# The level products of four recurrent heads: one group of 96 small matmuls on TensorE in place of two groups of 48

## The reference, cut to what matters

```python
def step(state, inp):
    qn, kn, vn, fn = inp
    b = jnp.cumsum(fn, axis=2)
    inter = jnp.einsum('bhtk,bhkv->bhtv', qn * jnp.exp(b), state)
    diff = b[:, :, :, None, :] - b[:, :, None, :, :]
    decay = jnp.exp(jnp.where(causal, diff, 0.0)) * causal_f
    a = jnp.einsum('bhtk,bhtsk,bhsk->bhts', qn, decay, kn)
    o = inter + jnp.einsum('bhts,bhsv->bhtv', a, vn)
    b_last = b[:, :, -1:, :]
    state = (jnp.exp(b_last[:, :, 0, :])[..., None] * state
             + jnp.einsum('bhsk,bhsv->bhkv', kn * jnp.exp(b_last - b), vn))
```

## Time and profile before

| | |
|---|---|
| median of 3 runs | 2510.53 us (2509.77 to 2511.0) |
| the profiled execution's own time | 2509.97 us |
| its span in the trace | 2508.7 us |
| TensorE busy | 2502.2 us of the span |
| VectorE busy | 1358.9 us |
| ScalarE busy | 918.4 us |
| GpSimd busy | 149.5 us |
| the four heads that the change touches | 140 to 350 us of the span |

### The profile page before, as it was taken

One profiled execution on the slowest core, in us unless ns is written; L12 is line 12 of the kernel. 1 busy time (PEld: TensorE's weight loads), 2 busy tenths in 40 slices (PEclk: granted clock), 3 DMA queues, 4 the chain that ended last, 5 costly groups with the idle time before them and its releaser, 6 DMA issues.

```text
span 2508.7 us, 31305 instructions
## 1 busy us (share of the span) xinstructions
PE 2502.2 (100%) x12614; PEld 2075.9 (83%) x12614; DVE 1358.9 (54%) x2248; ACT 918.4 (37%) x1259; POOL 149.5 (6%) x195
## 2 busy tenths in 40 slices
PE   9999999999999999999999999999999999999999
PEld 8888888888888888888888888888888888888888
DVE  7557744567544555655443363485256555665425
ACT  6633325333332222322232253443344344544423
POOL 0011110012100000000001103200000000000001
PEclk9999999999999999999999999999999999999999
DMA  5333333333335666666443232236222243433432
GB/s 192 110 96 95 96 105 95 95 95 100 100 93 164 213 218 214 218 212 212 149 161 110 93 101 93 93 101 178 92 76 76 85 125 101 113 106 112 178 101 101
DMA packets 213633, 317.95 MB, mean 127 GB/s; under 512 B 66736, under 2 KB 69680, under 8 KB 212464
## 3 DMA queue, kind: packets, MB, share of 16 engines
q1 hardware_dynamic: 208592, 312.55, 40.2%
q0 software_dynamic: 4320, 2.99, 0.5%
q10 hardware_dynamic: 576, 0.42, 0.1%
HBM read 295.43 MB, written 8.39 MB: 121 GB/s over the span
## 4 chain that ended last, share of the span: by engine, by line
PE 100%; ACT 0%; DVE 0%; issue 0%; ACTq 0%; DVEq 0%
PE bank L366 94%; PE bank L1449 1%; PE bank L1450 1%; PE bank L1451 1%; PE bank L798 0%; PE bank L857 0%; PE bank L782 0%; PE bank L860 0%; PE bank L825 0%; PE bank L1841 0%; PE bank L1955 0%; PE bank L1953 0%; PE bank L1954 0%; PE bank L467 0%; ACT OT L2266 0%; PE bank L472 0%
## 5 line engine op out<-in xcount | busy, mean ns | idle before, releaser
L366 PE MATMUL bank<-XH,WH 128*128 128x512 f32 (+1 forms) x2776 | 1078.7, 390 | 0.0
L366 PE MATMUL bank<-XH,WL 128*128 128x512 f32 (+1 forms) x2776 | 1074.5, 389 | 0.0
L366 PE MATMUL bank<-XL,WH 128*128 128x512 f32 (+1 forms) x2776 | 1074.0, 389 | 0.0
L418 DVE TENSOR_TENSOR WL<-RAW,WH 128x1024 fp32r<-128x1024 f32 x430 | 530.1, 1234 | 760.6 <-ACT WH L395 760.0
L395 ACT CAST WH<-RAW 128x1024 fp32r<-128x1024 f32 x430 | 450.1, 1048 | 1113.4 <-PE bank L366 1102.2
L366 PEld LDWEIGHTS bank<-XH,WL 128*128 128x128 f32 x2776 | 521.0, 188 | 108.1 <-DVE WL L418 0.2
L366 PEld LDWEIGHTS bank<-XH,WH 128*128 128x128 f32 x2776 | 521.0, 188 | 107.7 <-ACT WH L395 0.2
L366 PEld LDWEIGHTS bank<-XL,WH 128*128 128x128 f32 x2776 | 521.2, 188 | 107.1 <-issue 0.5
L366 PE MATMUL bank<-WH,XL 128*128 128x512 f32 x384 | 149.4, 389 | 0.0
L366 PE MATMUL bank<-WH,XH 128*128 128x512 f32 x384 | 149.4, 389 | 0.0
L366 PE MATMUL bank<-WL,XH 128*128 128x512 f32 x384 | 149.4, 389 | 0.0
(11 more groups left out here) (351 smaller groups left out, 1882.7 us busy)
## 6 DMA issues: line engine op xcount, KB each, us to landing
RAW<-in_w_in SPq DMA_DIRECT2D x303, 512.0 KB, 3.8
AST<-in_w_ada SPq DMA_DIRECT2D x192, 256.0 KB, 4.1
RAW<-in_w_o SPq DMA_DIRECT2D x32, 512.0 KB, 3.7
RAW<-in_w_gate SPq DMA_DIRECT2D x32, 512.0 KB, 3.6
RAW<-in_w_out SPq DMA_DIRECT2D x32, 512.0 KB, 3.7
RAW<-in_w_a SPq DMA_DIRECT2D x16, 512.0 KB, 4.2
RAW<-in_w_b SPq DMA_DIRECT2D x16, 512.0 KB, 4.3
PT<-ZT SPq DMA_DIRECT2D x256, 32.0 KB, 1.9
```

Source lines behind the costliest of these rows:

```text
L366: ins = nc.tensor.matmul(bank[b][:, cols], l, r[:, cols], start=first, stop=final)
L418: nc.vector.tensor_tensor(low_of(m), RAW[:, m % NRAW], high_of(m).bitcast(F32), ALU.subtract).then_inc(lo.sem, lo.step(m))
```

## The change

For heads 0 to 3 (`JOINED`) all eight levels are computed at slot 8 in one group. Levels 0 to 3 share one bank and levels 4 to 7 the other. Levels 3 and 5 are packed into 64 columns each instead of 256 (`half_of_tiles`), so that a bank's 512 columns suffice: 192 + 256 + 64, and 256 + 64 + 64 + 128. Their takes become four instructions of 32 or 16 partitions (`take_half_of_tiles`) instead of one of 128. The rows of levels 5, 6 and 7 move to rows 4, 5 and 6 of YA, which the convolution writes only in the second half of the heads. The takes of levels 0 to 3 move behind the product group. VectorE's number of slots stays the same. Heads 4 to 7 keep the two groups.

```diff
@@ -754,7 +754,13 @@
     XX4 = sb("XX4", [512], F32, W0 + 98560)
     XQ = sb("XQ", [16, 48], F32, W0 + 98560)
 
-    def level_rows(lev):
+    JOINED = range(4)
+
+    def level_rows(hh, lev):
+        if hh in JOINED and lev > 4:
+            if hh < 4:
+                return YA[:, lev - 1]
+            return O[:, lev] if hh == 4 else (LF, KK, Q)[lev - 5][:, hh - 5]
         return XX4[:, :] if lev == 7 else XX[:, {2: 2, 3: 1, 4: 0, 5: 1, 6: 2}[lev]]
 
     QUERIES = XX[:, 1]
@@ -793,26 +799,36 @@
             T.wait_ge(dve, (yield dve, ("xl", hh, lev)))
             for n in range(16):
                 y = 32 * n % 128
-                t = level_rows(lev)[:, 32 * n:32 * n + 32]
+                t = level_rows(hh, lev)[:, 32 * n:32 * n + 32]
                 c = slice(at + 16 * n, at + 16 * n + 16)
                 ins = nc.tensor.matmul(b[y:y + 32, c].rearrange("p (n x) -> p n x", x=h), t,
                                        late(t, lev), start=True, stop=True, tile_position=(0, y))
             return ins
 
...
@@ -825,21 +841,33 @@
                 ins = nc.tensor.matmul(b[:, CH[c]], KT[:, c], VN[:, c, 128 * i:128 * i + 128], start=True, stop=True)
             ins.then_inc(side.sem, side.step(("sums", hh)))
 
-        yield from idle(3)
-        b = yield from product_bank((0, 1))
-        yield from pairs_and_diagonal(b)
-        b = yield from product_bank((2, 3))
-        yield from within_tiles(2, b, 0)
-        ins = yield from within_tiles(3, b, 256)
-        ins.then_inc(side.sem, side.step(("prod", hh, 3)))
-        yield
-        yield from idle(3)
-        b = yield from product_bank((4, 5))
-        yield from within_tiles(4, b, 0)
-        yield from within_tiles(5, b, 256)
-        b = yield from product_bank((6, 7))
-        yield from across_tiles(b)
-        ins = yield from across_halves(b)
+        if hh in JOINED:
+            yield from idle(7)
+            b = yield from product_bank((0, 1, 2, 3))
+            yield from pairs_and_diagonal(b)
+            yield from within_tiles(2, b, 192)
+            yield from half_of_tiles(3, b, 448)
+            b = yield from product_bank((4, 5, 6, 7))
+            yield from within_tiles(4, b, 0)
+            yield from half_of_tiles(5, b, 256)
+            yield from across_tiles(b, 320)
+            ins = yield from across_halves(b, 384)
+        else:
+            yield from idle(3)
+            b = yield from product_bank((0, 1))
+            yield from pairs_and_diagonal(b)
+            b = yield from product_bank((2, 3))
+            yield from within_tiles(2, b, 0)
+            ins = yield from within_tiles(3, b, 256)
+            ins.then_inc(side.sem, side.step(("prod", hh, 3)))
+            yield
+            yield from idle(3)
+            b = yield from product_bank((4, 5))
+            yield from within_tiles(4, b, 0)
+            yield from within_tiles(5, b, 256)
+            b = yield from product_bank((6, 7))
+            yield from across_tiles(b, 0)
+            ins = yield from across_halves(b, 64)
         ins.then_inc(side.sem, side.step(("prod", hh, 7)))
         yield
         yield from idle(3)
@@ -921,6 +949,7 @@
     def hgrn_dve(i, hh):
         half = hh // 4
         lf, kk, q, r = LF[:, i], KK[:, i], Q[:, i], RR[:, :]
+        early = ("prod", hh, 7 if hh in JOINED else 3)
 
         def take_diagonal():
             b = bank[banks["prod", hh, 0]]
...
+        def take_half_of_tiles(lev):
+            h = 1 << (lev - 1)
+            at = 448 if lev == 3 else 256
+            b = bank[banks["prod", hh, lev]]
+            V.wait_ge(side, (yield side, ("prod", hh, 7)))
+            V.wait_ge(dve, (yield dve, ("take", hh, lev - 1)))
+            for y in range(0, 128, 32):
+                rows = slice(y, y + 32)
+                if lev == 5:
+                    ins = nc.vector.tensor_copy(ATD[y:y + 16, :, y + 16:y + 32],
+                                                b[y:y + 16, at:at + 64].rearrange("p (c x) -> p c x", c=4))
+                    continue
+                src = b[rows, at:at + 64].rearrange("p (c n x) -> p c n x", c=4, x=h)
+                msk = late(MASK[rows, lev, rows], lev).unsqueeze(1).broadcast_to([32, 4, 16 // h, h])
+                ins = nc.vector.copy_predicated(
+                    ATD[rows, :, rows].rearrange("p c (n x) -> p c n x", x=2 * h)[:, :, :, h:], msk, src)
+            ins.then_inc(dve.sem, dve.step(("take", hh, lev)))
+
...
@@ -985,7 +1033,8 @@
             V.wait_ge(act, (yield act, ("up", hh, lev)))
             V.wait_ge(ev_d, (yield ev_d, (("q", half), i)))
             if lev > 4:
-                V.wait_ge(side, (yield side, ("prod", hh, 3)))
+                if hh not in JOINED:
+                    V.wait_ge(side, (yield side, ("prod", hh, 3)))
             elif hh % 4:
                 V.wait_ge(dve, (yield dve, ("o", hh - 1)))
             if lev == 1:
...
@@ -1012,10 +1061,10 @@
             nc.vector.tensor_tensor(vw(lf)[:, :, h:], vw(lf)[:, :, h:],
                                     vw(lf)[:, :, h - 1:h].broadcast_to([128, n, h]), ALU.add
                                     ).then_inc(dve.sem, dve.step(("b", hh, lev)))
-            if lev == 5:
+            if lev == 5 and hh not in JOINED:
                 yield from take_diagonal()
                 yield from take_pairs()
-            if lev == 6:
+            if lev == 6 and hh not in JOINED:
                 yield from take_within(2)
                 yield from take_within(3)
             yield
@@ -1032,18 +1081,33 @@
         nc.vector.transpose(ZK[:, :, :], KEYS[:, BEFORE_END].rearrange("p (b x) -> p b x", x=32)
                             ).then_inc(dve.sem, dve.step(("kt", hh)))
         yield
-        yield from take_within(4)
-        yield from take_within(5)
+        if hh in JOINED:
+            yield from take_diagonal()
+            yield from take_pairs()
+            yield from take_within(2)
+        else:
+            yield from take_within(4)
+            yield from take_within(5)
         yield
         V.wait_ge(act, (yield act, ("up", hh, 8)))
         V.wait_ge(side, (yield side, ("prod", hh, 7)))
         nc.vector.tensor_tensor(QUERIES[:, AFTER_START], q[:, AFTER_START], EE[:, 0, AFTER_START], ALU.mult
                                 ).then_inc(dve.sem, dve.step(("queries", hh)))
-        yield from take_across(6)
-        yield
-        yield from take_across(7)
-        yield
-        yield
+        if hh in JOINED:
+            yield from take_half_of_tiles(3)
+            yield from take_within(4)
+            yield
+            yield from take_half_of_tiles(5)
+            yield from take_across(6)
+            yield
+            yield from take_across(7)
+            yield
+        else:
+            yield from take_across(6)
+            yield
+            yield from take_across(7)
+            yield
+            yield
         V.wait_ge(side, (yield side, ("sums", hh)))
         b = bank[banks["sums", hh]]
         nc.vector.tensor_copy(ST[:, 0], b[:, CH[0]]).then_inc(dve.sem, dve.step(("state", hh, 0)))
```

More of the change, by code:

```diff
@@ L800, in within_tiles, with half_of_tiles, across_tiles, across_halves @@
             return ins
-        def across_tiles(b):
+        def half_of_tiles(lev, b, at):
+            h = 1 << (lev - 1)
+            T.wait_ge(dve, (yield dve, ("xl", hh, lev)))
+            for n in range(16):
+                y = 32 * (n % 4)
+                t = level_rows(hh, lev)[:, 32 * n:32 * n + 32]
+                c = slice(at + 16 * (n // 4), at + 16 * (n // 4) + 16)
+                nc.tensor.matmul(b[y:y + 32, c].rearrange("p (n x) -> p n x", x=h), t,
+                                 late(t, lev), start=True, stop=True, tile_position=(0, y))
+        def across_tiles(b, at):
             T.wait_ge(dve, (yield dve, ("xl", hh, 6)))
-            x = level_rows(6)
+            x = level_rows(hh, 6)
             for n in range(8):
                 c, p = n // 2, n % 2
-                tile_product(b, 64 * p + 32 * (c % 2), 32 * (c // 2),
+                tile_product(b, 64 * p + 32 * (c % 2), at + 32 * (c // 2),
                              x[:, 64 * n:64 * n + 32], x[:, 64 * n + 32:64 * n + 64])
-        def across_halves(b):
+        def across_halves(b, at):
             T.wait_ge(dve, (yield dve, ("xl", hh, 7)))
-            x = level_rows(7)
+            x = level_rows(hh, 7)
             for n in range(8):
                 c, p = n // 2, n % 2
-                ins = tile_product(b, 64 * (c % 2) + 32 * p, 64 + 64 * (c // 2),
+                ins = tile_product(b, 64 * (c % 2) + 32 * p, at + 64 * (c // 2),
                                    x[:, 64 * n - 32 * p:64 * n - 32 * p + 32], x[:, 128 * c + 64:128 * c + 128])
@@ L931, in take_diagonal @@
                 V.wait_ge(pool, (yield pool, "at0"))
-            V.wait_ge(side, (yield side, ("prod", hh, 3)))
+            V.wait_ge(side, (yield side, early))
             for y in range(0, 128, 32):
@@ L952, in take_within @@
```

(15 more changed lines are left out.)

## The result

The changed kernel takes 2516.9 us, the median of 10 runs (2515.29 to 2519.88), against 2510.12 for the kernel before in the same session (10 runs, 2509.77 to 2511.02). The ratio is 1.0027, with a 95% interval of 1.0017 to 1.0037: slower by 6.8 us, where 1.2 less was forecast. The scatter has grown as well, from 1.3 to 4.6 us.

What follows compares the result with a forecast made beforehand. TensorE's queue length was taken as the bound (busy 2502.2 of 2508.7 us). The profiled 2509.97 less 1.2 for four heads' change-overs gives 2508.8; with the median 0.56 above that execution, 2509.3 was forecast, range 2506.8 to 2513.2.

Steps and rivals of the forecast that it cites:

- The likeliest case: Whole kernel: joining saves 1.2 us on TensorE, for a median of 2509.3 us; chance 0.71.
- The change-over of 0.30 us a head: TensorE: exit of the first product group and entry of the second go, 0.10 + 0.11 + 0.09 us; 1.2 for four heads.
- The sum: Profiled execution 2509.97 us less 1.2 is 2508.8; the runs' median lies 0.56 above that execution, so 2509.3.
- rival 2: TensorE's instruction fetch too slow for joined groups of 384 records: 2511.7 us with two heads, 2514.1 with four; chance 0.11.
- no margin: Instruction fetch: a packet takes 1.2 us to move and lasts 1.2 us at 19 ns a matmul, so the durations are equal.
- The present groups show no such pause though some must cross a border: Argument against fetch starvation: the two groups at 1.70 us, for example, show no pause, though some groups must cross packet borders.
- Rival 1: TensorE's product groups: nothing saved, the change-over pauses reappear inside the joined group, costing 2.5 us; time 2510.5; chance 0.12.
- Rival 3: VectorE finishes level 7 or the states too late for TensorE's output matmuls: 2511.6 us, or 2518.5 for every head; chance 0.04.
- The costs of its takes: VectorE: four level 3 takes at 0.30 us, four level 5 copies at 0.22 to 0.30; 1.0 to 1.4 us more a head.
- Slots, bank waits, SyncE's and GpSimd's queues: Head stays 17 slots, no DMA added, key transfers and clearing no later, bank waits covered by slack: no cost on TensorE.

Runs made afterwards that it cites:

- the version with two groups: Changed kernel, but TensorE issues levels 0 to 3 at slot 4 and 4 to 7 at slot 8 again: 2510.37 us, ratio 1.0 to the kernel before.

## Why the prediction was wrong

**The likeliest case.** The change-over of 0.30 us a head was right in kind: the unpaused joined groups cost 2.14 to 2.46 us against 2.48, so they save 0.02 to 0.34 a head, on average 0.2. Joined where no border troubles them, four heads saved 0.8 us inside their groups where 1.2 was said; the median's 1.0 is within the interval of no change.

**Where the sum failed.** The sum, 2509.97 less 1.2, put the instruction supply at nothing. The text knew of it as rival 2, with a chance of 0.11 and a price that was too low, "at most one packet time, 1.2 us". The range did not even cover that price: it ends at 2513.2, and rival 2 with all four heads stood at 2514.1. I had worked out the time in which the DMA engines move a packet, and set it against the 1.2 us in which a packet is used up. From there the two seemed equal, hence "no margin" but a small price. The runs show that the packet is the smaller part of a refill. From its landing to the next instruction are 1.3 to 1.5 us more, and it starts late besides. The next instruction came 3.3 to 4.9 us after the start of the group, while within the burst the block in hand is used up after 1.4 to 1.8. Inside a group the pause is 1.9 to 3.0 us, 1.6 to 2.5 times the price that I gave as its highest. The second missing term is the clock: nothing in the trace of before shows TensorE pausing, so I did not price what a pause does to it. Its half clock costs 1.0 to 1.65 us and stood behind 8 of 14 pauses. In the profiled execution head 0 costs 2.9 us more than before, head 3 1.75 and the half clock 1.6, while heads 1 and 2 save 0.6: 5.7 together, against a span 5.5 longer. The median lies 1.3 us further off; no trace shows those executions, and their pauses or half clock are not known singly.

**Where the chances failed.** "The present groups show no such pause though some must cross a border" was taken for evidence. It is none: a group of 192 instructions can cross at most one border, and the block behind it is already there. Only a group longer than 256 can use up the next one as well within its burst. The arithmetic for this stood in the text (192 against 384), and should have given this rival more than 0.11, and the position of each group in the stream could have been counted. Two of four heads, as it said, were struck.

The page of the Trainium skill, "Runtime: NRT & Kernel Launch" (Instruction fetch mechanics), was read as undecided between a store of 2048 instructions and two lines of 256. The pauses decide it for this kernel: each comes exactly one block after the border whose refill is awaited, so no more than one block was in hand. The same section says that the fetch is hidden since instructions are dispatched more slowly than the blocks are filled. The trace disagrees for this stream, in which 192 instructions leave in 1.0 us and a refill takes 3.3 us or more.

**Rival 1** falls by the traces: it wanted a joined group at 2.5 us, and the unpaused ones cost 2.14 to 2.46, 2.27 on average. The times alone can't tell it from the forecast. **Rival 3** falls as well, by the version with two groups and by VectorE's idle 2.54 us ahead of the states. The costs of its takes were right or high (0.22 us for all eight new small ones, against 0.22 to 0.30). Slots, bank waits, SyncE's and GpSimd's queues cost nothing, as said: that version is equal to the kernel before.

**What stays open.** Why the packet starts 1.0 us into a group in one place and 2.5 in another; why the clock falls behind some pauses and not behind others of the same length; and why unpaused groups differ by 0.3 us (2.14 with the border at 145 or 177, 2.44 to 2.46 at 6, 26 or 250, 2.25 to 2.27 at the others).

## What to carry to other kernels

Count instructions, not only microseconds, where an engine is fed with very short ones: here a run of more than about 256 small TensorE instructions (64 f32 matmuls) without 2.7 us of long ones in between can starve on its instruction fetch, by 2 to 3 us and sometimes 1.0 to 1.65 more in clock. (The 2.7 us are one case; how little would do was not tried.) Whether it does depends on where the run falls modulo 256, so an edit far ahead of it can bring the loss or take it away; a small saving by a longer burst needs its place counted. No group of 192 paused in any trace here. And an idle time of an otherwise full engine whose releaser is "issue" should be looked for in the timeline, since a busy share of 100% hides it.

## What the runs showed of the hardware

- TensorE's instructions come in blocks of 256 here (14 pauses in six kernels, each ending at the same remainder), and with one block in hand a refill takes 3.3 to 4.9 us from the start of the burst to the next instruction: 0.9 to 1.5 us for the 16 KB packet, 1.3 to 1.5 after its landing, the rest before it starts.
- Dense matmuls of 512 columns last 29 us a block (256 / 2 x 0.2265), so they never show it, except in the stretch just behind a burst (the pause at 266.95).
- Behind 8 of the 14 pauses, of 1.96 to 3.0 us, TensorE's granted clock was 0.50 for some 3 us (1.2 of 2.4 GHz) and then full again, at a price of 1.0 to 1.65 us. Behind the other six, of 1.26 to 2.92 us, it stayed full.
- A predicated copy of 32 x 64 took 0.22 us in level 3 and 0.29 in the pairs' take, both four at a time; a plain copy of 16 x 64 took the same 0.22 as one of 32 x 64.
